# Attention copies ahead of the exponentials, and a filter's vector steps dealt more thinly over a projection

## The chip, the cores and the metric

One Trainium2 chip, one of its cores. The metric is the device time of one execution in microseconds (us). All data are float32. The engines are named as the profile names them: PE (TensorE), DVE (VectorE), ACT (ScalarE), POOL (GpSimd), SP (SyncE, here used to issue transfers).

## The reference

Two residual blocks run one after the other on x (1 x 2048 x 1024).

```
# first block
h = rmsnorm(x); q, k, v, g_a, u_p, g_p = split(h @ w_in)
a = banded_attention(q, k, v, rel_bias, sink) * silu(g_a)   # 8 heads, 2 kv heads, 128-token blocks, 3 blocks of keys
p = multiscale_pool(u_p) * silu(g_p)
x = x + rmsnorm(concat(a, p) @ w_out)
# second block
h = rms_norm(x); x0, x1, v (short conv of 3 taps), hy_gate, sg_u, sg_v, sg_gate = split(h @ w_in_2)
f = sin(fr1 * (z @ w1 + b1)); f = sin(fr2 * (f @ w2 + b2)); f = sin(fr3 * (f @ w3 + b3)); k = filter from f @ w_o
y_a = x0 * long_conv(v * x1, k) * silu(hy_gate)
y_b = sg_u * (per-head 128x128 mix of normalised sg_v) * silu(sg_gate)
x = x + rms_norm(concat(y_a, y_b) @ w_out_2)
```

The frequencies of the filter's sines are large, so its second layer (64 inputs, 64 outputs, 2048 positions) is computed in compensated float32 arithmetic on DVE, not on PE. The third layer is a matmul, behind the second layer's sine.

## The kernel before, in words

The stages follow one another: normalisation and projections of the first block; attention; output product of the first block; the values of the gating unit in the second block; the tiles of the second block's projection; the long convolution; the output product. Everything is one hand-written program for each engine, ordered by semaphores.

**Attention.** There are 32 steps `STEPS`, one for each block of 128 queries and each group of four heads. PE's program for step st, in order, is: two heads' probabilities turned (`turned(0)`, `turned(1)`, transposes at L859, behind `probs_done`), the products with the values of step st-1 (`products`, L880), two more heads turned, and the scores of step st+3 (`scores`, L783). DVE's is: `softmax_out(st)` (L682 to L685, it divides by the sums and ends with the long multiply of L685), `softmax_in(st+2)` (four reads of scores, L666, then the negated maxima, L670 and L671) and `gate(st-2)` (L693). ACT copies the turned probabilities out of PSUM, one copy for each of four heads (L535), and computes the exponentials of step st+2 (`exponentials`, four at L471 with their sums and a small one at L473). The turned heads share two PSUM banks, so a head is turned only when the copy of the head two before it is done.

**The projection's tiles.** A list `tiles` is walked by all engines. First, for h of 0 to 7: `gate` h, `mix` h, `u` h. Then, for e of 0 to 7: `x0` e, `hgate` e, `x1` e, `v` e; the tile `third` (the filter's third layer) stands in this list too. All but `mix` and `third` are projection tiles: 96 matmuls of 512 columns (L1836 to L1838) into four PSUM banks, two sets of banks taking turns. So tile j needs the banks of tile j-2 (`banks_free`) and its low weights WL. DVE makes the low weights of the tile two ahead (L1721) behind its own work on tile j: two products for `mix` (L1767, L1771), one for `u` (L1762) and `hgate` (L1778), two outer taps for `x0`, `x1` and `v` (L1731, L1734), a product more for `v` (L1775). Before that, ACT empties the tile (Silu, or the middle tap of L1706) and makes the high weights (L1663).

Behind its own work on a tile, DVE does some of the 631 steps of the filter's second layer, each on 128x1024 elements (L120 to L143): `SV_OPS` deals 60 of them to the stage before, and `OPS_BY` says how many go behind each kind of tile. At one tile DVE does all that are left and then `second_angle` (L1739 to L1741 and `reduce_angle`), for which ACT's sine (L1674) and then the tile `third` (L1820) wait. Behind `third` DVE does `third_angle` (L1745 to L1749), and ACT two sines (L1677, L1678) ahead of its work on `hgate` 7.

In the first 24 tiles there is a chain of transfers too: when DVE has done `u` h, SP stores it (L1631, 1 MB), and only then does POOL load the values of `mix` h+1 (L1657, 1 MB) into the same part of SBUF.

Of the kernel before, what the change touches and what calls it, by code (L numbers as in the profile page):

```python
# [13 lines left out]
P = 128  # L14
# [60 lines left out]
def OPS_OF(rows):  # L75

    return 10 * rows - 9
# [73 lines left out]
def first_block(nc, ctx, A, M, WOH, WOL, FH, FL, PS, kept, x1_d, h1_d, h2_d, wv_d):  # L151
# [60 lines left out]
    def turned_keys(slot, r, n):  # L212
        base, step = ((45056 + 2 * W_KEYS * (r % 2), W_KEYS), (47616 if r % 2 else 31744, 832 if r % 2 else W_KEYS))[slot]
        return M[:, base + step * (r // 2):base + step * (r // 2) + n]
# [98 lines left out]
    def keys_of(n):  # L313
        return [kb for kb in (n - 1, n, n + 1) if 0 <= kb < NT]

    def cols_of(n):
        ks = keys_of(n)
        return (ks[0] - n + 1) * P, (ks[-1] - n + 2) * P

    STEPS = [(n, g) for n in range(NT) for g in range(2)]  # L320
# [128 lines left out]
    def first_scalar(s, ahead_of_scale, ahead_of_square, behind_square):  # L449
# [15 lines left out]
        def exponentials(st):  # L465
            n, g = STEPS[st]
            c0, c1 = cols_of(n)
            st_sm = SM[:, st % 3]
            s.wait_ge(negmax_done, st + 1)
            for r in range(4):  # L470
                s.activation(SC[:, st % 3, r, c0:c1], SC[:, st % 3, r, c0:c1], ACT.Exp,  # L471
                             bias=st_sm[:, 1, r:r + 1], accum_out=st_sm[:, 2, r:r + 1]).then_inc(exp_done, 1)
            s.activation(st_sm[:, 3], st_sm[:, 3], ACT.Exp).then_inc(exp_done, 1)  # L473
# [42 lines left out]
        def weights_high(k):  # L516
            s.activation(WOH[:, k], WOL[:, k].bitcast(F32), ACT.Copy).then_inc(woh_done, 1)

        def features_high(i):
            s.wait_ge(attn_done, 2 * i + 2)  # L520
            s.wait_ge(pt_in[i % 2], 16 * (i // 2 + 1))
            if i >= 2:
                s.wait_ge(mix_done, i - 1)
            s.activation(FH[:, i % 2, 0:4], GA[:, :, P * i:P * i + P], ACT.Copy).then_inc(fh_done, 1)
            s.activation(FH[:, i % 2, 4:8], FL[:, i % 2, 4:8].bitcast(F32), ACT.Copy).then_inc(fh_done, 1)

        for st, (n, g) in enumerate(STEPS):
            for r in range(4):
                if r == 2 and st + 2 < len(STEPS):
                    exponentials(st + 2)  # L530
                s.wait_ge(pT_done, 4 * st + r + 1)
                if st >= 2:
                    s.wait_ge(pv_done, st - 1)
                nk = P * len(keys_of(n))
                s.activation(turned_keys(st % 2, r, nk), PS[:, 4 + r % 2, 0:nk], ACT.Copy).then_inc(pT_read, 1)  # L535
            if st == len(STEPS) - 2:
                s.wait_ge(wo_in, 16 * KD)
                s.wait_ge(scores_done, len(STEPS))
                features_high(0)
                weights_high(0)  # L540
# [623 lines left out]
def second_inputs(nc, A, PS, first, first_ctx, CC, HP, kept, h1_d, h2_d, vn_d, bi_d, u_d, gx_d, yb_d, wv_d):  # L1164

    with ExitStack() as outer:
# [75 lines left out]
        def rows_behind(sp, a, n):  # L1242

            for q in range(a, min(a + n, OPS_OF(HID))):
                r = row_used_by(q)
                if r is not None and r + 4 < ROWS_OF(HID):
                    row_load(sp, r + 4)
            return min(a + n, OPS_OF(HID))

        w_cols = []  # L1250
        tiles = []
        for h in range(8):
            tiles += [("gate", h, 6144 + P * h), ("mix", h, None), ("u", h, 4096 + P * h)]
        for e in range(8):
            if e == 7:
                tiles.append(("third", 0, None))
            tiles += [("x0", e, P * e), ("hgate", e, 3072 + P * e), ("x1", e, 1024 + P * e), ("v", e, 2048 + P * e)]
        weights = [j for j, t in enumerate(tiles) if t[2] is not None]
        slot_of = {j: w for w, j in enumerate(weights)}
        wv2 = A["w_in_2"].rearrange("(k p) e -> p k e", p=P)  # L1260
# [5 lines left out]
        with ExitStack() as ctx:  # L1266
# [18 lines left out]
            STEPS = 2 * NT  # L1285
# [284 lines left out]
        with ExitStack() as ctx:  # L1570
# [26 lines left out]
            third = tiles.index(("third", 0, None))  # L1597
            NV = 8

            def evacs_before(j):  # L1600

                return sum(t[0] not in ("u", "mix") for t in tiles[:j])
# [8 lines left out]
            def _(sp):  # L1611
                values_sync(sp)

                def raw_next(w):
                    if w + 2 < len(weights):
                        sp.wait_ge(wl_done, NV + w + 1)
                        weight_load(sp, w + 2)
# [10 lines left out]
                for j, (kind, n, _) in enumerate(tiles):  # L1628
# [9 lines left out]
                    if j in slot_of and slot_of[j] + 2 < len(weights):  # L1638
                        raw_next(slot_of[j] + 2)
                    a = rows_behind(sp, a, OPS_BY[kind])  # L1640

# [18 lines left out]
            def _(s):  # L1660
# [8 lines left out]

                values_scalar(s, first_high)  # L1670
                for j, (kind, n, _) in enumerate(tiles):
                    if j == third - 1:
                        s.wait_ge(arg2_done, 1)
# [39 lines left out]
            def _(v):  # L1713
# [10 lines left out]
                def outer_taps(which, n, j):  # L1724

                    conv = 3 * n + which
                    ps = PS[:, 4 * (j % 2):4 * (j % 2) + 4, :].rearrange("p a b -> p (a b)")
                    dst = AB[CONV_AT[CONV[which]]]
                    w = CW[:, 8 * which + n]
                    v.wait_ge(evac_done, evacs_before(j) + 1)  # L1730
                    v.scalar_tensor_tensor(out=dst[:, 1:S], in0=ps[:, 0:S - 1], scalar=w[:, 0:1], in1=dst[:, 1:S],  # L1731
                                           op0=ALU.mult, op1=ALU.add).then_inc(tap_step, 1)
                    v.wait_ge(tap_step, conv + 1)
                    v.scalar_tensor_tensor(out=dst[:, 0:S - 1], in0=ps[:, 1:S], scalar=w[:, 2:3], in1=dst[:, 0:S - 1],  # L1734
                                           op0=ALU.mult, op1=ALU.add).then_inc(taps_done, 1)
                    v.wait_ge(taps_done, conv + 1)
# [6 lines left out]
                def third_angle(j):  # L1743
                    v.wait_ge(evac_done, evacs_before(j) + 1)
                    link(v.tensor_scalar(L3[0], L3[0], VEC3[:, 0:1], VEC3[:, 1:2], ALU.add, ALU.mult))  # L1745
                    v.wait_ge(tile_done, j + 1)
                    reduce_angle(link, v, L3[0], L3[1], L3[2])
                    v.tensor_scalar(L3[1], L3[1], -3.1415925, 3.1415925, ALU.max, ALU.min).then_inc(arg3_done, 1)
                    v.memset(L3[2][HID:P, 0:1], 0.0).then_inc(arg3_done, 1)  # L1749
# [7 lines left out]
                for j, (kind, n, _) in enumerate(tiles):  # L1757
                    ps = PS[:, 4 * (j % 2):4 * (j % 2) + 4, :].rearrange("p a b -> p (a b)")
                    if kind == "u":
                        v.wait_ge(tile_done, j + 1)  # L1760
                        v.wait_ge(mix_gated, n + 1)
                        v.tensor_tensor(AB[n % 2], ps, AB[n % 2], ALU.mult).then_inc(sgu_done, 1)  # L1762
                    elif kind == "mix":
                        v.wait_ge(tile_done, j + 1)
                        v.wait_ge(sgt_in[n % 2], 32 * (n // 2 + 1))
                        psb = PS[:, 4 * (j % 2):4 * (j % 2) + 4, :].rearrange("p a (b c) -> p (a b) c", c=P)
                        v.scalar_tensor_tensor(out=psb, in0=psb, scalar=NW[:, n:n + 1], in1=BI[:, n % 2].unsqueeze(1).to_broadcast([P, NT, P]),  # L1767
                                               op0=ALU.mult, op1=ALU.add).then_inc(mix_biased, 1)
                        v.wait_ge(mix_biased, n + 1)
                        v.wait_ge(evac_done, evacs_before(j))  # L1770
                        v.tensor_tensor(AB[n % 2], ps, AB[n % 2], ALU.mult).then_inc(mix_gated, 1)  # L1771
                    elif kind in CONV:
                        outer_taps(CONV.index(kind), n, j)
                        if kind == "v":
                            v.tensor_tensor(AB[1], AB[0], AB[1], ALU.mult).then_inc(u_done, 1)  # L1775
                    elif kind == "hgate":
                        v.wait_ge(evac_done, evacs_before(j) + 1)
                        v.tensor_tensor(AB[0], AB[0], AB[1], ALU.mult).then_inc(gx_done, 1)  # L1778
                    elif kind == "third":
                        third_angle(j)  # L1780
                    if j in slot_of and slot_of[j] + 2 < len(weights):
                        weights_low(slot_of[j] + 2)
                    if (kind, n) == ("x0", 6):
                        filter_work(v, OPS_OF(HID))
                        second_angle()
                    else:
                        filter_work(v, OPS_BY[kind])
                v.wait_ge(sin3_done, 2)
# [53 lines left out]


SV_OPS = [0] * 8 + [3] * 20 + [0] * 4
OPS_BY = {"gate": 12, "u": 13, "mix": 6, "x0": 13, "hgate": 13, "x1": 13, "v": 13, "third": 0}


def reduce_angle(link, v, x, out, tmp):
# [1006 lines left out]
```

## Time and profile before

| | before |
|---|---|
| median of 3 runs | 3157.5 us (3156.0 to 3157.89) |
| the profiled execution: its time | 3156.89 us |
| the profiled execution: its span | 3154.8 us |
| PE, DVE, ACT busy in the span | 2986.2, 2543.4, 814.3 us |
| attention, start of the first L685 to start of the last | 578.9 to 736.2 us |
| the projection's tiles, first matmul to last | 1144.9 to 2259.6 us |

Busy time is the time in which an engine has an instruction in flight; PE's matmuls overlap, so a busy PE is not a PE at its fastest. The distance from one matmul's start to the next tells more. A row's idle time stands in brackets, with what ended it.

### The profile page before, as it was taken

The page shows a single profiled execution, that of the slowest core. Times are in us where ns is not written, and L with a number is a line of the kernel's source. Part 1 is how long each engine was busy: PE and PEld are TensorE (multiplying, and loading weights), DVE is VectorE, ACT ScalarE, POOL GpSimd, SP SyncE. Part 2 cuts the span into 40 slices and gives each one's busy share as a digit, 9 for nine tenths or more (in the row PEclk, how much of TensorE's full clock was granted, in tenths as well). Part 3 has the DMA queues.
Part 4 walks back from the last instruction along what each step waited for, and adds up shares of the span by engine and source line. Part 5 has one row for each costly group of instructions (what it writes and reads, how often), then busy time and mean ns, then how long its engine had stood idle before and what let it go on. Part 6 is the DMA issues. An engine that isn't in the chain of part 4 may idle for free. (4 is left out here: it accounts for less than half of the span.)

```text
span 3154.8 us, 32979 instructions
## 1 busy us (share of the span) xinstructions
PE 2986.2 (95%) x12866; PEld 2164.8 (69%) x12866; DVE 2543.4 (81%) x2789; ACT 814.3 (26%) x1370; POOL 336.1 (11%) x458
## 2 busy tenths in 40 slices
PE   8999999889998999999999999998889989889999
PEld 4444444656777888888888887776656656678887
DVE  7979999898996869999999999996368879762121
ACT  3000000585334220000011111111344626631111
POOL 2212121001343430000000000000000000000000
PEclk9999999999999999999999999999999999999999
DMA  7675552201457546565555445431222331453331
GB/s 213 182 179 149 172 151 73 114 1 57 143 186 237 146 135 167 157 184 153 155 140 140 127 140 147 134 100 47 97 91 66 123 112 56 147 167 115 99 107 41
DMA packets 212116, 406.39 MB, mean 129 GB/s; under 512 B 21009, under 2 KB 134329, under 8 KB 204089
## 3 DMA queue, kind: packets, MB, share of 16 engines
q1 hardware_dynamic: 189256, 324.58, 34.0%
q0 software_dynamic: 21552, 71.32, 8.3%
q10 hardware_dynamic: 1152, 8.39, 0.7%
q8 instruction: 102, 1.67, 0.2%
q14 instruction: 54, 0.43, 0.0%
HBM read 324.53 MB, written 85.98 MB: 130 GB/s over the span
## 5 line engine op out<-in xcount | busy, mean ns | idle before, releaser
L1836 PE MATMUL PS<-HX,WH 128*128 128x512 f32 x1536 | 602.4, 392 | 23.1 <-DVE WL L1721 15.1
L1838 PE MATMUL PS<-HX,WL 128*128 128x512 f32 x1536 | 600.0, 391 | 0.0
L1837 PE MATMUL PS<-HX,WH 128*128 128x512 f32 x1536 | 599.9, 391 | 0.0
L843 PE MATMUL PS<-M 128*128 128x512 f32 x1088 | 472.0, 596 | 7.6 <-DVE M L644 6.4
L843 PEld LDWEIGHTS PS<-M 128*128 128x128 f32 x1088 | 207.4, 191 | 272.0 <-issue 263.7
L1836 PEld LDWEIGHTS PS<-HX,WH 128*128 128x128 f32 x1536 | 290.0, 189 | 88.3 <-issue 15.8
L1838 PEld LDWEIGHTS PS<-HX,WL 128*128 128x128 f32 x1536 | 289.8, 189 | 60.7
L1837 PEld LDWEIGHTS PS<-HX,WH 128*128 128x128 f32 x1536 | 290.0, 189 | 59.7
L120 DVE SCALAR_TENSOR_TENSOR HP<-MF,HP 128x1024 f32<-128x1024 f32 x252 | 323.4, 1283 | 8.0
L120 DVE SCALAR_TENSOR_TENSOR M<-M 128x1024 f32<-128x1024 f32 x160 | 205.5, 1285 | 26.6 <-DMA M<-c_feat 21.1
L2523 PE MATMUL PS<-WH,YH 128*128 128x512 f32 x512 | 201.9, 394 | 9.3 <-DVE HP L2662 5.2
L2524 PE MATMUL PS<-WH,YL 128*128 128x512 f32 x512 | 200.9, 392 | 0.0
L2525 PE MATMUL PS<-WL,YH 128*128 128x512 f32 x512 | 200.9, 392 | 0.0
L2646 DVE TENSOR_TENSOR YL<-KX,YH 128x2048 fp32r<-128x2048 f32 x14 | 32.1, 2291 | 206.7 <-ACT YH L2625 206.7
L1706 ACT ACTIVATE MB<-PS,MF 128x2048 f32<-128x2048 f32 x24 | 49.6, 2065 | 475.2 <-PE PS L1838 392.2
L2053 POOL DMA_DIRECT2D M<-c_decay x48 | 25.8, 538 | 1112.5 <-DVE KX L2167 909.0
L72 POOL DMA_DIRECT2D M<-c_feat x186 | 94.9, 515 | 382.6 <-DVE M L120 361.9
L2523 PEld LDWEIGHTS PS<-WH,YH 128*128 128x128 f32 x512 | 97.3, 190 | 31.7 <-issue 7.1
L1521 PE MATMUL PS<-WVH,HX 128*128 128x512 f32 x256 | 102.5, 400 | 13.9 <-DVE HX L1445 6.0
L1020 DVE TENSOR_TENSOR M<-M 128x1024 f32<-128x1024 f32 x90 | 110.1, 1223 | 2.4
L2525 PEld LDWEIGHTS PS<-WL,YH 128*128 128x128 f32 x512 | 97.1, 190 | 20.6
L2524 PEld LDWEIGHTS PS<-WH,YL 128*128 128x128 f32 x512 | 97.4, 190 | 20.0
(223 smaller groups left out, 5048.9 us busy)
## 6 DMA issues: line engine op xcount, KB each, us to landing
MF<-h_scratch SPq DMA_DIRECT2D x380, 256.0 KB, 4.3
M<-c_feat POOLq DMA_DIRECT2D x186, 256.0 KB, 4.4
MF<-w_in SPq DMA_DIRECT2D x52, 512.0 KB, 4.8
M<-u_scratch SPq DMA_DIRECT2D x16, 1024.0 KB, 4.8
M<-c_decay POOLq DMA_DIRECT2D x48, 256.0 KB, 2.9
M<-x SPq DMA_DIRECT2D x18, 512.0 KB, 4.2
M<-w_in SPq DMA_DIRECT2D x18, 512.0 KB, 5.5
x_scratch<-M SPq DMA_DIRECT2D x16, 512.0 KB, 5.1
```

The costliest lines, as they stand in the source:

```text
L72: eng.dma_start(dst[HID * half:HID * half + HID], row).then_inc(loaded, 16)
L120: return v.scalar_tensor_tensor(out=out, in0=a, scalar=s_, in1=b, op0=op0, op1=op1)
L843: ins = t.matmul(ps[:, c, :], wt[:, k], HT[:, k, TC * c:TC * c + TC], start=(k == 0), stop=(k == KD - 1))
L1020: link(v.tensor_tensor(out, a, b, op))
L1521: t.matmul(dst, hh, wh, start=(k == 0), stop=False)
L1706: s.activation(AB[CONV_AT[kind]], ps, ACT.Identity, bias=w[:, 3:4], scale=w[:, 1:2]).then_inc(evac_done, 1)
L1836: t.matmul(dst, wh, hh, start=(k == 0), stop=False)
L1837: t.matmul(dst, wh, hl, start=False, stop=False)
L1838: ins = t.matmul(dst, wl, hh, start=False, stop=(k == KD - 1))
L2523: t.matmul(dst, yh, wh, start=(n == 0), stop=False)
L2524: t.matmul(dst, yl, wh, start=False, stop=False)
L2525: return t.matmul(dst, yh, wl, start=False, stop=(n == KY - 1))
```

## The change

Two things are changed. In attention, ACT makes all four copies of a step and then the exponentials of step st+2; before, the exponentials stood between the second copy and the third. In the projection, `u`, `x0` and `x1` take 12 filter steps instead of 13, `v` takes 11 and `hgate` 14. The tile at which DVE does what is left, and then the second angle, is `x1` 6 instead of `x0` 6. The tile `third` stands behind `x0` 7 instead of ahead of it.

```diff
@@ first_scalar
             for r in range(4):
-                if r == 2 and st + 2 < len(STEPS):
-                    exponentials(st + 2)
                 s.wait_ge(pT_done, 4 * st + r + 1)
                 if st >= 2:
                     s.wait_ge(pv_done, st - 1)
                 nk = P * len(keys_of(n))
                 s.activation(turned_keys(st % 2, r, nk), PS[:, 4 + r % 2, 0:nk], ACT.Copy).then_inc(pT_read, 1)
+            if st + 2 < len(STEPS):
+                exponentials(st + 2)
@@ second_inputs
         for e in range(8):
+            tiles.append(("x0", e, P * e))
             if e == 7:
                 tiles.append(("third", 0, None))
-            tiles += [("x0", e, P * e), ("hgate", e, 3072 + P * e), ("x1", e, 1024 + P * e), ("v", e, 2048 + P * e)]
+            tiles += [("hgate", e, 3072 + P * e), ("x1", e, 1024 + P * e), ("v", e, 2048 + P * e)]
@@
-                    if (kind, n) == ("x0", 6):
+                    if (kind, n) == ("x1", 6):
                         filter_work(v, OPS_OF(HID))
                         second_angle()
@@
-OPS_BY = {"gate": 12, "u": 13, "mix": 6, "x0": 13, "hgate": 13, "x1": 13, "v": 13, "third": 0}
+OPS_BY = {"gate": 12, "u": 12, "mix": 6, "x0": 12, "hgate": 14, "x1": 12, "v": 11, "third": 0}
```

## Rows read from the trace of the kernel before

**Rows 1.** Waits, 578 to 731 us: us in total, times, longest.
```profile
PE PS L859 <- ACT M L535: 19.6, 29, 1.7
DVE M L666 <- PE PS L783: 6.1, 14, 1.6
```
**Rows 2.** Timeline of ACT in one step: start, us, instruction, idle before.
```profile
703.25 0.62 ACT L471 ACTIVATE M<-M 128x384 f32<-128x384 f32 x1 [0.51 <-DVE M L671]
...
705.76 0.84 ACT L535 ACTIVATE M<-PS 128x384 f32<-128x384 f32 x2
```
**Rows 3.** Timeline of PE in the same stretch.
```profile
701.32 0.85 PE L859 MATMUL PS<-M 128*128 128x128 f32 x6 [0.79 <-ACT M L535]
...
703.54 0.87 PE L859 MATMUL PS<-M 128*128 128x128 f32 x6
704.34 1.56 PE L783 MATMUL PS<-M 64*128 64x384 f32 x8
```
**Rows 4.** Timeline of DVE in the same stretch.
```profile
698.81 1.76 DVE L685 TENSOR_TENSOR M<-M 128x1536 f32<-128x1536 f32 x1
...
703.87 1.76 DVE L685 TENSOR_TENSOR M<-M 128x1536 f32<-128x1536 f32 x1
705.95 0.62 DVE L666 CUSTOM_DVE_ANT_0 M<-PS,M 128x384 f32<-128x384 f32 x1 [0.33 <-PE PS L783]
```
**Rows 5.** Waits, 731 to 746 us.
```profile
DVE M L666 <- PE PS L783: 0.5, 1, 0.5
PE PS L859 <- ACT M L535: 2.4, 2, 1.8
```
**Rows 6.** Source view of L1767 (`mix`): first and last start.
```profile
L1767 DVE SCALAR_TENSOR_TENSOR PS<-PS,MF,MB x8: 2357/2359/2359, 1186.5 to 1529.9; 128x2048 f32<-128x2048 f32 x8
```
**Rows 7.** Timeline of DVE: twelve filter steps behind `gate` 0.
```profile
1171.05 1.22 DVE L143 TENSOR_TENSOR MF<-HP,MF 128x1024 f32<-128x1024 f32 x1
...
1186.53 2.36 DVE L1767 SCALAR_TENSOR_TENSOR PS<-PS,MF,MB 128x2048 f32<-128x2048 f32 x1
```
**Rows 8.** Source view of L1706 (ACT, middle tap), 1550 to 1820 us.
```profile
L1706 ACT ACTIVATE MB<-PS,MF x10: 2065/2067/2069, 1556.8 to 1817.9; 128x2048 f32<-128x2048 f32 x10
```
**Rows 9.** Source view of L1731 (DVE, first tap), 1740 to 2110 us.
```profile
L1731 DVE SCALAR_TENSOR_TENSOR MB<-PS,MF,MB x13: 2349/2349/2351, 1743.0 to 2104.4; 128x2047 f32<-128x2047 f32 x13
```
**Rows 10.** Timeline of PE: `mix` 1, `mix` 7 with the next tile, `x0` 0.
```profile
1216.31 0.91 PE L1813 MATMUL PS<-MB 128*128 128x128 f32 x6 [2.18 <-DMA MB<-vn_scratch]
...
1507.93 3.81 PE L1813 MATMUL PS<-MB 128*128 128x128 f32 x32 [0.28 <-DMA MB<-vn_scratch]
1511.50 0.47 PE L1836 MATMUL PS<-HX,WH 128*128 128x512 f32 x1
...
1534.68 0.50 PE L1836 MATMUL PS<-HX,WH 128*128 128x512 f32 x1 [1.15 <-DVE MB L1771]
```
**Rows 11.** Timeline of SP: the stores of `u` 0 and `u` 6.
```profile
1201.18 0.33 SPq L1631 DMA_DIRECT2D yb_scratch<-MB  x1
...
1495.45 0.34 SPq L1631 DMA_DIRECT2D yb_scratch<-MB  x1
```
**Rows 12.** Waits of PE, 1534.6 to 2163 us.
```profile
PE PS L1836 <- DVE WL L1721: 13.2, 6, 6.1
```
**Rows 13.** Timeline of PE: `third` and the tile behind it.
```profile
2163.14 1.97 PE L1820 MATMUL PS<-MF 64*64 64x512 f32 x16
2170.12 0.80 PE L1836 MATMUL PS<-HX,WH 128*128 128x512 f32 x1 [5.02 <-DVE MB L1734]
```
**Rows 14.** Timeline of DVE: second angle, third angle, what follows each.
```profile
2124.46 0.81 DVE L1739 TENSOR_SCALAR MF<-MF 128x1024 f32<-128x1024 f32 x1
...
2135.13 2.28 DVE L1778 TENSOR_TENSOR MB<-MB 128x2048 f32<-128x2048 f32 x1
...
2173.45 1.34 DVE L1745 TENSOR_SCALAR MF<-MF 128x2048 f32<-128x2048 f32 x1
...
2192.79 0.06 DVE L1749 MEMSET HP<- 64x1 f32 x1
```

## The prediction, as it was put on record

> **What bounds the kernel now.** The change touches two stretches, attention (578.9 to about 738 us) and the projection's tiles (1144.9 to 2259.6), so I read each by itself: first the waits of the stretch, then a timeline of each engine over one period, then the view of one instruction, whose first and last start give the length of a period.
>
> In attention the three engines are all nearly full. Two waits matter [rows 1]: PE waits for ACT's copies 29 times, 19.6 us in all, and DVE waits for PE's scores 14 times, 6.1 us in all. One period shows how they hang together. ACT computes exponentials from 703.25 to 705.76 and only then makes the copies of the third and fourth head [rows 2]. PE turns the next head only when such a copy is done: at 701.32 it had sat 0.79 us. From there to the end of its scores it takes 704.34 + 1.56 - 701.32 = 4.58 us, so to 705.90 [rows 3]. DVE ends its long multiply at 703.87 + 1.76 = 705.63 and starts on the scores at 705.95, after 0.33 idle [rows 4]. Without that idle time its period is 703.87 - 698.81 = 5.06 us. So DVE sets the pace, and every second step PE is a third of a microsecond late, because of ACT's order.
>
> In the projection the period of DVE and that of PE have to be compared. PE: ACT's first tap follows the end of a tile at once where PE is not held up, and x0 0 to x0 3 is 12 tiles in 1817.9 - 1556.8 = 261.1, so 21.76 a tile and 87.0 for the four tiles of an e [rows 8]. DVE: between the taps of x0 2 and of x0 6 lie four periods, (2104.4 - 1743.0) / 4 = 90.35 [rows 9]. DVE is the slower by 3.3 us an e; PE first eats its lead and then waits for low weights, 13.2 us in 6 waits [rows 12]. For the 24 tiles in front: DVE's period over an h is (1529.9 - 1186.5) / 7 = 49.06 [rows 6]; PE's is two tiles and a mix, 2 x 21.76 + (1511.50 - 1507.93) = 47.09 [rows 10]. Here too DVE is the slower, and x0 0 starts at 1534.68 behind the second product of mix 7, whose banks it needs [rows 10]. So through the projection the bound is DVE, until its filter steps run out; from there PE.
>
> **The change, part by part.**
>
> A filter step costs DVE (1186.53 - 1171.05) / 12 = 1.29 us [rows 7].
>
> First, u takes 12 instead of 13. DVE's period over an h falls to 47.77, still above PE's 47.09. Seven deals of u stand in front of mix 7's products, so they end 7 x 1.29 = 9.0 earlier, at 1525.7 by DVE alone. By PE alone it would be 1144.9 + 16 x 21.76 + 8 x 3.57 = 1521.6. A third limit is the chain u, store, load, mix. From the store's issue to the mix it took 1216.31 - 1201.18 = 15.1 at mix 1 and 1507.93 - 1495.45 = 12.5 at mix 7 [rows 10, 11]. Say PE ends gate h at 0. High and low weights are ready some 3.3 + 1.1 later (evacuation 2.1, high 1.1, low 1.1, the durations of like operations), twelve steps take 15.5, the two products 4.6, six steps 7.7, u's product 2.2: 34.5. With the chain behind it, mix h+1 may start at 47.0 to 49.6, where PE comes at 47.1. A mix that is late holds PE, but not DVE's steps, so the next chain starts no later and only every second wait is a new one. At a chain of 13.8 (the mean) this costs 1.5 us over the stretch beyond DVE's limit. I take x0 0 at 1527.2, 7.5 earlier. With all chains at 12.5 it is 9; with all at 15.1 PE's period is (47.1 + 49.6) / 2 = 48.4 and the gain is about 2.5.
>
> Second, the tiles of an e take 12 + 14 + 12 + 11 = 49 steps instead of 52. DVE's period becomes 90.35 - 3 x 1.29 = 86.5, below PE's 87.0: PE is the bound, and does not wait for weights any more. What it lost is the distance between two of its own rows less the tiles in it: from 1534.68 to third at 2163.14 [rows 10, 13] stand 28 tiles, 28 x 21.76 = 609.3 of 628.5. The loss was 19.2 us (15 of idle time, 4 of matmuls at twice their distance behind it, TensorE's lower clock). I count all of it as gained. If DVE kept some lag, it would be less; the margin is 0.5 us an e, so I put the lower bound at 12.
>
> Third, the steps left over. Before: 8 x 31 + 6 x 52 = 560 of the 571 that the tiles have to do, so 11 at x0 6. After: 8 x 30 + 6 x 49 + 12 + 14 = 560, so 11 at x1 6. PE ends x1 6 at 1527.2 + 27 x 21.76 = 2114.7. DVE: first tap at 2116.9, both taps to 2121.7, low weights of x0 7 at 2122.8, eleven steps to 2137.0, second angle (2135.13 - 2124.46 = 10.7 [rows 14]) to 2147.7. Before, it was the next tile but one that wanted weights queued behind the angle, 6.1 us of wait [rows 12]; now DVE has little lag, and the weights of x0 7 stand ahead of the eleven steps. Queued behind the angle are v 6's taps (to 2152.4) and the sine of ACT; third comes at 2114.7 + 2 x 21.76 = 2158.2. So 5.8 us of cover, and it costs nothing.
>
> Fourth, third behind x0 7. Before, the tile behind third waited for the taps of v 6, which PE had just finished: 2170.12 - 2163.14 = 7.0 from third's start [rows 13]. Now hgate 7 waits for the taps of x0 7 in the same way: the same 7.0, and the slow matmuls behind it too. Nothing gained, nothing lost. Third angle (2192.79 - 2173.45 = 19.3 [rows 14]) now ends at 2158.2 + 7.0 + 1.1 + 19.3 = 2185.6, ACT's two sines at about 2189.7, as PE ends hgate 7 at 2189.0. Its emptying is late by a microsecond; who waits for it is the last v, by its banks and low weights, from 2211 on. Cover: 15 us. SP's row loads move with the steps; each is issued a dozen steps ahead as before.
>
> Fifth, attention. With the copies first, PE can begin a pass at the end of the probabilities, 700.57 instead of 701.32, and its scores end at 705.2, 0.4 before DVE wants them. I count DVE's waits for scores, less the 1.6 us one in front, which is behind another tile: 4.5, and 0.5 at the end [rows 1, 5]. At the end PE loses another 1.8 us to ACT [rows 5]; there the last exponentials come 1.3 later but PE starts earlier: I take 1.0 of 0 to 2. What waits now is the exponentials. From the start T of a pass, heads three and four are turned from T + 2.2 to 3.1 (703.54 [rows 3]), copied to T + 3.9, exponentials to T + 6.4. DVE asks for them at T + 7.8: cover 1.4. Behind them stand the first two copies of the next step, ready at T + 6.9 and 7.3; PE wants them for its third and fourth head at T + 5.1 + 2.2 = 7.3 and 7.7. Cover 0.4, the tightest place. Sum 6.0 us, bounds 0 and 7.5.
>
> **Sum.** 7.5 + 19.2 + 6.0 = 32.7. The profiled execution took 3156.9 (2.1 around its span of 3154.8), so 3124.2; the median of the runs is 0.6 above it. Prediction 3125. Between the stretches and behind them nothing hangs on a fixed time, so what is gained stays.
>
> **Rivals.**
>
> The chain of transfers decides in the first 24 tiles. For it: it varies by 2.6 us, and row loads run beside it. Against: at mix 7 it took 12.5 and the wait was 0.28 [rows 10]. It gives 15.1 throughout, a gain of 2.5 for 7.5, so 3130. The Trainium skill ("DMA: Bandwidth & Descriptors", Issuing engines are not separate DMA queues) says that transfers of SP and POOL end on the same 16 DMA engines and interleave. By that rule the row loads, hardly fewer than before, keep slowing POOL's load, and this rival is the outcome.
>
> Attention gains nothing: the cover of 0.4 is not there and the step stays at 5.2 on average. 3131.
>
> DVE stays the bound in the e tiles: 12 instead of 19.2 is gained there. 3132; together with one of the others some 3137.
>
> Slower: ACT's exponentials behind the copies become attention's bound. Each microsecond that the first copies come later than PE wants them is one in each of 30 steps. To undo 26.7 it takes 0.9 a step, so copies 1.3 later than reckoned; at 1.2 a step it is 3157.5 - 26.7 + 36 = 3167. Against: ACT's own loop is 2.5 of exponentials and 1.7 of copies, with some 0.4 between, 4.6 of the 5.06.
>
> **How the numbers follow.** Forecast 0.70 (3125; its own range 3120 to 3130), chain 0.11 (3130), attention without gain 0.08 (3131), DVE still the bound 0.07 (3132 to 3137), slower 0.03 (3167), and 0.01 for no change. The range is 3119 to 3134. A measurement of this kernel tells some 0.2% (6 us) from no change. Faster by more 0.95, within 0.02, slower 0.03.
>
> **What would show it.** DVE's idle time before L666 gone and L685 every 5.06 us; PE's waits for low weights gone between x0 0 and third; ACT's first taps every 87.0 for an e up to x1 6; x0 0 near 1521 (attention's 6 less); third some 33 us earlier and a wait of 5 behind it. Wrong would be a PE that waits for copies in attention, or for L1721 again, or longer for vn_scratch.

## The result, and the profile after

The changed kernel takes 3132.3 us (median of 4 runs, 3128.7 to 3135.0), against 3156.75 us before in the same comparison (4 runs, 3155.8 to 3157.9). The ratio is 0.9922, with a 95% interval of 0.9905 to 0.9939: 24 us, or 0.8%, faster. Forecast were 3125 and a range of 3119 to 3134.

The profiled execution took 3128.7 us, with a span of 3126.9. Line numbers of the projection and behind it are one higher than before, and the copies of turned probabilities are L533 instead of L535. Attention's waits, in the stretch that answers to [rows 1]:

```profile
ACT M L533 <- PE PS L859: 26.4, 32, 1.4
PE PS L859 <- DVE M L685: 12.8, 30, 1.6
...
DVE M L666 <- PE PS L783: 1.6, 1, 1.6
```

But for 0.3 us once, TensorE no longer waits for ACT's copies in this stretch. ACT waits for TensorE, TensorE for the probabilities of VectorE, and VectorE for scores only once, at the start. The pace is in the view of the probabilities' multiply L685: 25 of them, first and last start.

```profile
L685 DVE TENSOR_TENSOR M<-M x25: 1757/1757/1759, 604.3 to 722.8; 128x1536 f32<-128x1536 f32 x25
```

That is (722.8 - 604.3) / 24 = 4.94 us a step (4.96 each, the last one 4.43). The same 25 of the kernel before:

```profile
L685 DVE TENSOR_TENSOR M<-M x25: 1757/1757/1759, 604.9 to 729.2; 128x1536 f32<-128x1536 f32 x25
```

5.18 a step. The first 24 tiles of the projection: TensorE's waits in the kernel before, then in the changed one, and the view that answers to [rows 6]:

```profile
PE PS L1813 <- DMA MB<-vn_scratch: 7.1, 6, 2.5
PE PS L1836 <- DVE MB L1771: 2.9, 4, 1.2
```

```profile
PE PS L1814 <- DMA MB<-vn_scratch: 6.8, 7, 1.8
PE PS L1837 <- DVE WL L1722: 1.9, 1, 1.9
```

```profile
L1768 DVE SCALAR_TENSOR_TENSOR PS<-PS,MF,MB x8: 2359/2359/2359, 1176.3 to 1514.1; 128x2048 f32<-128x2048 f32 x8
```

The waits for VectorE's mix product are gone, but all seven mixes with a predecessor waited for the stored values, and the period is (1514.1 - 1176.3) / 7 = 48.26, not VectorE's 47.77 of the prediction. In the e tiles (ACT's and VectorE's first taps, as [rows 8] and [rows 9]):

```profile
L1707 ACT ACTIVATE MB<-PS,MF x10: 2065/2067/2069, 1542.2 to 1803.4; 128x2048 f32<-128x2048 f32 x10
```

```profile
L1732 DVE SCALAR_TENSOR_TENSOR MB<-PS,MF,MB x13: 2349/2350/2351, 1719.1 to 2067.2; 128x2047 f32<-128x2047 f32 x13
```

TensorE's 12 tiles take 261.2, and VectorE's period is (2067.2 - 1719.1) / 4 = 87.03: both are at TensorE's pace now. From 1541 to 2152 us TensorE has no wait at all. The only one behind it in the projection is that of the tile after `third`, as [rows 13]:

```profile
PE PS L1837 <- DVE MB L1735: 5.0, 1, 5.0
```

By first instructions the profiled execution gained 10.2 us up to the projection (its first matmul 1144.94, now 1134.72) and 22.8 in the projection, so the convolution starts 33.0 earlier (2269.64, now 2236.61). Then 5.2 are given back: from there to the output's first matmul it takes 504.0 instead of 498.8. Behind that the kernels take the same 386.

### The profile page after: what moved, and what is told of

The parts are those of the page before. It is cut to its first block and busy times, and to the rows that moved or that the text cites. A ratio compares the mean times of both kernels' runs of the same rounds, so it can differ in the third digit from the quotient of the medians.

```text
span 3126.9 us, 32982 instructions
## 1 busy us (share of the span) xinstructions
PE 2980.9 (95%) x12866; PEld 2162.9 (69%) x12866; DVE 2541.6 (81%) x2789; ACT 811.2 (26%) x1370; POOL 335.9 (11%) x458
## 3 DMA queue, kind: packets, MB, share of 16 engines
q8 instruction: 102, 1.67, 0.2%
## 5 line engine op out<-in xcount | busy, mean ns | idle before, releaser
L72 POOL DMA_DIRECT2D M<-c_feat x186 | 94.9, 515 | 382.6 <-DVE M L120 361.9
```

The costliest lines, as they stand in the source:

```text
L72: eng.dma_start(dst[HID * half:HID * half + HID], row).then_inc(loaded, 16)
```

## The experiments

Each comparison below is with the kernel before in runs on the same chip. To keep the parts apart I name for most runs the time from the projection's first matmul to ACT's first tap of x0 0, called the **first part** (411.8 before, 407.5 in the changed kernel's first profile), and the length of the convolution.

**Attention alone.** Before, with this:

```
             for r in range(4):
-                if r == 2 and st + 2 < len(STEPS):
-                    exponentials(st + 2)
...
+            if st + 2 < len(STEPS):
+                exponentials(st + 2)
```

> Only the attention's part of the change. My theory: the gain is DVE's, whose period falls from 5.21 on average to 4.96 us, so the projection's first matmul comes 10.2 us earlier than before (8.6 of it by the end of attention), and the kernel takes 3146 to 3148 us. Rival (the 10.2 are shared with the projection's stage, which starts from another point): 6 us, 3151. If the long convolution loses TensorE clock by where it happens to start, as it did in the changed kernel (5.1 us), the time can be up to 5 us above the theory's with the projection still 10.2 us earlier.

3149.97 us (10 runs; before 3157.45), ratio 0.9978 (0.9969 to 0.9987). The step is 4.94 us as in the changed kernel. Counted from the first scores, the first matmul of attention's output projection comes 8.4 us earlier than before (8.3 in the changed kernel's profile). Counted from the first probabilities, the projection's first matmul comes 9.7 earlier, between the 10.2 of the theory and the 6 of the rival. The projection was as before (first part 412.1). The median is 2 us above the theory's range. In this profile the convolution took 501.6 us, 2.8 more than before, which the expectation had allowed for.

**Projection alone.** The tile order, the place of the second angle and the deals, with attention as before:

```
         for e in range(8):
+            tiles.append(("x0", e, P * e))
             if e == 7:
                 tiles.append(("third", 0, None))
...
-                    if (kind, n) == ("x0", 6):
+                    if (kind, n) == ("x1", 6):
...
-OPS_BY = {"gate": 12, "u": 13, "mix": 6, "x0": 13, "hgate": 13, "x1": 13, "v": 13, "third": 0}
+OPS_BY = {"gate": 12, "u": 12, "mix": 6, "x0": 12, "hgate": 14, "x1": 12, "v": 11, "third": 0}
```

> Only the projection's part. Theory: the stage from its first matmul to its last becomes 22.8 us shorter, 4 of it ahead of x0 0 and 19.2 behind it, and DVE never makes PE wait for low weights; the convolution starts 22.8 us earlier, the kernel takes 3134 us. Rival: with a late convolution clock, 3134 to 3139. If the parts helped each other, their gains alone would add up to less than 33.0 at the start of the convolution.

3137.73 us (4 runs; before 3157.45), ratio 0.9939 (0.9924 to 0.9954). The first part took 410.0 and the whole projection 1103.2 instead of 1124.7. TensorE waited 9.3 us for the stored values. Expected were 22.8 us in the projection, 4 of it in the first part; it was 21.5, with 1.8 in the first part. The two parts' ratios add to 0.83%, about the 0.78 of the whole.

**The thinner deals without the moved angle and layer.** Attention as changed, new deals, `third` ahead of x0 7 and the second angle at x0 6, where all leftover steps now fall. The deals are those of the edit above, and SP's row loads follow the leftover:

```
-                    a = rows_behind(sp, a, OPS_BY[kind])
+                    a = rows_behind(sp, a, OPS_OF(HID) if (kind, n) == ("x0", 6) else OPS_BY[kind])
```

> Attention's part and the thinner deals, but DVE does what is left (37 steps instead of 11) and the second angle at x0 6 still, and third stays ahead of x0 7; SP issues the rows of all those steps there. Theory: what was spread is paid back in one wait. 26 steps more than before, 33.5 us, stand ahead of the low weights of v 6, with only the lag gained as cover: a wait of some 27 us at v 6 instead of 6, the projection's stage 3 us longer to 1 us shorter than before, the kernel 3145 to 3150 us. Rival (thinner deals alone bring the gain, and the place of the angle is of no matter): 3128 to 3133.

3160.1 us (10 runs; before 3157.45), ratio 1.0012 (1.0002 to 1.0021), with attention's gain in it. Its waits of TensorE from 1134 to 2275 us:

```profile
PE PS L1836 <- DVE WL L1721: 29.0, 2, 27.1
PE PS L1813 <- DMA MB<-vn_scratch: 10.3, 6, 2.5
```

The steps that were taken off the tiles pile up at one tile, with the angle behind them, and the weights of the next tile but one come 27.1 us late in one wait, as expected. But the kernel is 10 us above the expected 3145 to 3150. Its projection, from its first matmul to the convolution's, is 10.3 us longer than before (1135.0 for 1124.7) instead of 3 at most: the first part took 412.5 and gained nothing, and the matmuls behind the long wait ran at twice their distance. The deals save time only if the leftover has a tile with room for it.

**Third layer ahead of x0 7 again,** all the rest as changed:

```
         for e in range(8):
-            tiles.append(("x0", e, P * e))
             if e == 7:
                 tiles.append(("third", 0, None))
+            tiles.append(("x0", e, P * e))
```

> The changed kernel with the third layer ahead of x0 7 again, all the rest as changed: second angle at x1 6, new deals. If the later angle needs the third layer one tile later, TensorE waits at the third layer for the sine: the angle is ready about a tile and a half before, so 10 to 18 us are lost there, the half clock behind the wait costs 2 to 3 more, and the kernel takes 3142 to 3155. Rival, the order of these two tiles is worth nothing (the sine is ready in time either way): 3130 to 3135, and no wait of TensorE on the sine over 1 us.

3147.74 us (4 runs; before 3158.26), ratio 0.9957 (0.994 to 0.9973). Its waits of TensorE from 1138 to 2262 us:

```profile
PE PS L1821 <- ACT MF L1675: 12.5, 1, 12.5
PE PS L1814 <- DMA MB<-vn_scratch: 11.6, 4, 3.4
```

The sine is waited for 12.5 us, and the sixteen short matmuls behind that wait take 3.29 us where they took 1.97 [rows 13]. So moving the third layer by a tile is needed as soon as the angle is later. The rest of this run's time is the other wait, and the profile shows its rhythm in mixes 1 and 3:

```profile
1209.78 5.24 PE L1814 MATMUL PS<-MB 128*128 128x128 f32 x32 [2.44 <-DMA MB<-vn_scratch]
...
1308.95 3.25 PE L1814 MATMUL PS<-MB 128*128 128x128 f32 x15 [3.27 <-DMA MB<-vn_scratch]
```

Mix 2 between them had no wait: only every second late chain is a new one. And the 32 matmuls behind the first wait take 5.24 us, where they take 3.81 at the full clock [rows 10]. So it is with all four mixes that waited (5.15 to 5.44 us), 5.8 us in all. This run's first part took 417.4 us, ten more than the changed kernel's, by the same code up to there.

**The chain of transfers taken off the path.** The changed kernel with other deals:

```
-OPS_BY = {"gate": 12, "u": 12, "mix": 6, ...
+OPS_BY = {"gate": 12, "u": 18, "mix": 0, ...
```

The six steps between the mix's products and u's product go behind u's product, so u is stored up to six steps (7.7 us) earlier, with the same work ahead of the next mix's products.

> The changed kernel with mix 0 and u 18 instead of mix 6 and u 12: the six steps stand behind u's product, so its store and the load of the next mix's values start some 7 us earlier, and DVE has as much to do as before. Theory (in the changed kernel the chain of transfers, not DVE, sets the pace of the first 24 tiles): PE's seven waits for vn_scratch go, x0 0 starts 3 to 5 us earlier, the kernel 3 to 5 us shorter. Rival (DVE sets it): the waits for vn_scratch turn into waits for DVE and nothing is gained.

3124.91 us (4 runs; before 3157.45), ratio 0.99 (0.9883 to 0.9916). The first part took 405.2, 2.3 us less than in the changed kernel's first profile (expected were 3 to 5). The waits for stored values are gone, and a small one on VectorE's mix product is there instead. Run again:

> The version with no filter steps at a mix tile and 18 at a u tile once more, beside the next two: 3122 to 3128, and a projection of 1099 us from its first matmul to the convolution's first. If only the convolution's share moves between executions, the projection stays within 0.7 us of 1099.2 and the convolution lies anywhere from 498 to 505.

3122.76 us (4 runs; before 3157.94), ratio 0.9888 (0.9872 to 0.9905), first part 405.2 and the projection 1099.2 both times, and the convolution 499.1 and 499.3. So the expectation held. TensorE's wait in the second one:

```profile
PE PS L1837 <- DVE MB L1772: 4.2, 7, 0.8
```

**One step fewer at u, and its step dealt to hgate.**

```
-OPS_BY = {"gate": 12, "u": 12, "mix": 6, "x0": 12, "hgate": 14, ...
+OPS_BY = {"gate": 12, "u": 17, "mix": 0, "x0": 12, "hgate": 15, ...
```

> The changed kernel with deals of 0 at mix, 17 at u (12 at gate as before), 15 at hgate. In the version with 18 at u TensorE waited 4.1 us in 7 waits for VectorE's mix product, and for no transfer. If VectorE's work is what bounds the first 24 tiles there (29 steps of 1.29 us a group in place of 30), these waits go, 3.5 to 4.1 us less up to x0 0, and no wait on the stored values appears as there is still about 18 us of cover for 15: 3118 to 3124. Rival, the transfers are next: VectorE comes to the mix product 1.3 us earlier, the row is waited for instead, and 0 to 1 us is gained: 3122 to 3128.

3121.13 us (4 runs; before 3157.94), ratio 0.9882 (0.9867 to 0.9897), the fastest kernel here (the next one, with 3121.47, is as fast within the noise). Its first part took 399.0 us, 12.9 less than before. The products of the mix stand 47.19 us apart, TensorE's own period (47.09) but for 0.1:

```profile
L1768 DVE SCALAR_TENSOR_TENSOR PS<-PS,MF,MB x8: 2359/2359/2360, 1180.1 to 1510.4; 128x2048 f32<-128x2048 f32 x8
```

and in the whole first part TensorE has one wait left, for the first low weights (1.9 us). SP stores u 0 at 1188.26 and the mix begins at 1207.50, with no wait before it:

```profile
1188.26 0.33 SPq L1632 DMA_DIRECT2D yb_scratch<-MB  x1
```

```profile
1207.50 3.73 PE L1814 MATMUL PS<-MB 128*128 128x128 f32 x32
```

So 19.2 us from the store's issue to the mix, where the changed kernel had 14.2 and a wait of 1.25:

```profile
1190.95 0.33 SPq L1632 DMA_DIRECT2D yb_scratch<-MB  x1
```

```profile
1205.14 3.81 PE L1814 MATMUL PS<-MB 128*128 128x128 f32 x32 [1.25 <-DMA MB<-vn_scratch]
```

Against the version with 18 at u the first part is 6.2 us shorter (expected were 3.5 to 4.1), but only 2.6 of it are left at the convolution: x0 0 to `third` takes 1.9 longer, by a wait of 1.8 for v 6's taps, and the tile behind `third` waits 7.3 instead of 5.0. Those taps stand behind the second angle in VectorE's queue, and VectorE gets no sooner through its steps because TensorE is ahead (this is read from the order of the queue; no run moved the angle here).

**The same with 13 steps at x0,** which leaves 5 for the angle's tile instead of 12.

> The same with 13 steps at x0 instead of 12, which leaves 5 for the tile of the second angle instead of 12. If the wait of 5.0 us of TensorE behind VectorE's taps late in the projection comes from the leftover steps and the angle, it shrinks to 0 to 2 us and the kernel gains 3 to 5 us on the one before it; if VectorE has no room for a 51st step in a group of four tiles, TensorE waits 1.3 us in each and the gain is gone again: 3118 to 3128.

3121.47 us (4 runs; before 3157.94), ratio 0.9882 (0.9868 to 0.9897): no change. The wait behind `third` is 7.0 instead of 7.3, so a smaller leftover does not shorten it. VectorE has the same number of steps up to the angle however they are dealt.

**Exponentials behind three copies.**

```
             for r in range(4):
+                if r == 3 and st + 2 < len(STEPS):
+                    exponentials(st + 2)
                 s.wait_ge(pT_done, 4 * st + r + 1)
...
-            if st + 2 < len(STEPS):
-                exponentials(st + 2)
```

> The changed kernel with the exponentials of a step behind three copies of the step before instead of behind all four. Theory of the prediction, what counts is that the copies of turned probabilities don't queue behind the exponentials: TensorE waits for the fourth copy at the end of the exponentials once a step, so the gain is a part only, a step of 5.0 to 5.3 us, the last probabilities 0 to 4 us later than in the changed kernel (152.0 us from first to last there, 157.3 before), and the end of attention up to 3 us later still by the fourth copy of the last step but one. Whole 3127 to 3135. Rival, any place behind the second copy will do: 152.0 us and 8.6 us gained by the output of attention, as in the changed kernel, whole as there.

3157.54 us (10 runs; before 3157.94), ratio 0.9997 (0.9988 to 1.0006). Both expectations missed, by over 20 us. The step is neither 4.94 nor 5.2:

```profile
L685 DVE TENSOR_TENSOR M<-M x26: 1224/1757/1759, 606.7 to 753.5; 128x1536 f32<-128x1536 f32 x25, 128x1024 f32<-128x1024 f32 x1
```

(753.5 - 606.7) / 25 = 5.87, and the long steps take 5.92. ACT, one step of it:

```profile
696.11 0.49 ACT L535 ACTIVATE M<-PS 128x384 f32<-128x384 f32 x1 [1.44 <-PE PS L859]
696.49 0.61 ACT L471 ACTIVATE M<-M 128x384 f32<-128x384 f32 x1
...
698.98 0.84 ACT L535 ACTIVATE M<-PS 128x384 f32<-128x384 f32 x2
700.09 0.49 ACT L535 ACTIVATE M<-PS 128x384 f32<-128x384 f32 x1 [0.26 <-PE PS L859]
```

TensorE and VectorE in the same stretch (the three waits return in every step):

```profile
697.82 0.55 PE L859 MATMUL PS<-M 128*128 128x128 f32 x3
699.50 0.55 PE L859 MATMUL PS<-M 128*128 128x128 f32 x3 [1.14 <-ACT M L535]
```

```profile
697.93 0.62 DVE L666 CUSTOM_DVE_ANT_0 M<-PS,M 128x384 f32<-128x384 f32 x1 [0.87 <-PE PS L783]
```

ACT waits 1.44 for the third head to be turned, starts 2.5 us of exponentials in front of the fourth copy, and TensorE can't turn the next step's second head until that copy has emptied the bank that the two share. So TensorE's next scores are late by 1.14, VectorE waits 0.87 for them, and its maxima and the exponentials behind them are late in turn: a closed ring of three engines. In the kernel before, ACT began its exponentials as soon as VectorE's maxima let it, at 703.25 [rows 2], and had both late copies behind them; here it waits for the third head first, and everything behind is later by that. From the first probabilities to the projection's first matmul it takes 566.0 us with exponentials behind two copies, 583.1 behind three, and 556.0 to 557.1 behind four (the changed kernel's two profiles; 564.1 to 566.0 and 556.0 to 558.9 over all profiles with two and with four).

**The changed kernel once more.**

> The changed kernel as it is, once more, for the convolution. In its profile 17 to 18 of the 128 first-stage matmuls of the filter columns ran at 0.85 us instead of 0.43, against 7 in the kernel before, and the convolution took 504.0 us against 498.8. Theory A, the granted clock falls by where the kernel happens to stand in time, and differs from execution to execution: another count of slow matmuls in this profile, and a convolution of 499 to 507 us. Theory B, the loss belongs to the new kernel: the same counts by chunk, 4, 4, 5, 4, and 503.7 to 504.3 us.

3128.02 us (2 runs; before 3158.26), ratio 0.99 (0.988 to 0.992). The convolution took 499.2, not 504.0, with 0, 5, 5, 5 slow matmuls in its four chunks. (Counted are distances over 0.7 us between the 32 matmuls of a chunk; in the second to fourth chunk a wait of 2.3 us counts as one of them, so a 1 means that none was slow.) The same code took 4.8 us less in another execution, so the loss is not the code's own. Windows of TensorE over the convolution: stretch, its length, busy time and instructions, granted clock, DMA share, GB/s. First profile of the changed kernel:

```profile
2236.00:2284.00 48.00, 41.18 (x190) 0.90 0.46 176
...
2364.00:2390.00 26.00, 21.06 (x64) 0.93 0.06 21
2390.00:2492.00 102.00, 95.20 (x488) 0.98 0.34 120
...
2646.00:2741.00 95.00, 82.72 (x371) 0.94 0.37 133
```

The same kernel in this run:

```profile
2240.00:2288.00 48.00, 40.71 (x193) 0.93 0.50 187
...
2368.00:2394.00 26.00, 21.57 (x71) 0.93 0.07 21
2394.00:2496.00 102.00, 94.62 (x494) 1.00 0.34 120
...
2650.00:2741.00 91.00, 79.15 (x347) 0.96 0.37 134
```

Three of the four stretches shown got more clock. In the second one, the first stage of the second chunk, both lost it, and the kernel before, which stood elsewhere in time, did not:

```profile
2397.00:2423.00 26.00, 21.39 (x80) 1.00 0.07 21
```

**The convolution shifted in time,** by VectorE operations at the projection's end that write a tile nobody reads any more, four of them in the changed kernel, then two in the kernel before:

```
                 v.wait_ge(sin3_done, 2)
+                for _ in range(4):
+                    link(v.tensor_tensor(MISS, ACC, ACC, ALU.add))
```

> The changed kernel with four VectorE operations of 1.26 to 1.32 us more at the end of the projection, behind the wait for the third sine, where the convolution waits for them: they write a tile that nobody reads any more. Both theories: the convolution's first matmul 5.0 to 5.3 us later than in the changed kernel. Theory A, the loss hangs on where in time the convolution stands: the counts of slow matmuls by chunk change, and the convolution takes 497 to 503 us or over 505. Theory B, the loss belongs to the kernel's new code: 4, 4, 5, 4 stay, the convolution takes 503.7 to 504.3 us and the whole 3133 to 3140.

3140.79 us (2 runs; before 3158.26), ratio 0.9941 (0.9921 to 0.996). The shift itself was 4.7 us, a little under the expected 5.0 to 5.3. The slow matmuls are 4, 1, 4, 1 and the convolution took 501.5, which theory A allows and B does not. The rest of the loss is in the first part, 413.0 us in this run.

> The kernel before with two VectorE operations more at the same place, 2.5 to 2.6 us in all. Both theories: first matmul of the convolution 2.5 to 2.6 us later. Theory A: counts of slow matmuls other than 4, 1, 1, 1, and a convolution that is up to 5 us longer than 498.8, the whole up to 3165. Theory B: 4, 1, 1, 1 stay, 498.5 to 499.1 us, and the whole 3160.

3160.56 us (8 runs; before 3158.26), ratio 1.0008 (0.9998 to 1.0019). Shifted by 2.1 us (expected 2.5) the kernel before has the counts 0, 5, 5, 4, as the changed one had in other runs, yet a convolution of 499.2: what the first stage lost, other stretches won. Over the 14 profiles of this study the convolution took 498.7 to 504.0 us, and 504.0 came once, in the first profile of the changed kernel.

## Why the prediction came out as it did

Faster was right, and both medians of the changed kernel, 3132.3 and 3128.0, lie in the range of 3119 to 3134, 7 and 3 us above the forecast. The mechanism was right for attention and for the e tiles. In the first 24 tiles it was not: there the rival held.

**Attention, forecast 6.0 (0 to 7.5): 8.5 in the first two profiles, some 7.2 against the others.** That DVE sets the pace and loses its waits was right. The step was taken as 5.06 and is 4.96: in the kernel before DVE began to read the scores 1.77 us after the start of its multiply even where no wait is listed (698.81 to 700.58), and in the changed kernel after 1.67. The last probabilities are 5.4 us earlier (730.82, before 736.20), 5.2 counted from the first ones, against a forecast of 4.5 and 0.5 at the end. For the end itself, "I take 1.0 of 0 to 2", 3.1 us came (first matmul of the output product 736.73, before 745.24). In the kernel before the last exponentials stood in front of the third and fourth copy of the last step but one. TensorE of the kernel before, then of the changed one:

```profile
736.27 0.72 PE L859 MATMUL PS<-M 128*128 128x128 f32 x4 [1.82 <-ACT M L535]
736.92 2.15 PE L880 MATMUL PS<-M 128*64 128x256 f32 x12
739.00 2.27 PE L859 MATMUL PS<-M 128*128 128x128 f32 x8
```

```profile
732.10 0.66 PE L859 MATMUL PS<-M 128*128 128x128 f32 x4 [0.69 <-DVE M L685]
732.69 1.08 PE L880 MATMUL PS<-M 128*64 128x256 f32 x8
734.14 0.71 PE L859 MATMUL PS<-M 128*128 128x128 f32 x4 [0.37 <-ACT M L533]
```

I had counted the 1.8 of idle time, but not that the products of that step came behind it, nor the slow matmuls that followed it: 12 take 2.15 us, where in the middle of attention they take 1.52, and 8 take 2.27 where four take 0.71 in the changed kernel. These slow matmuls belong to that execution and not to the order of the copies. In the run of the kernel before with a shifted convolution the wait is the same 1.82 and the 12 stand at full clock:

```profile
736.87 0.72 PE L859 MATMUL PS<-M 128*128 128x128 f32 x4 [1.82 <-ACT M L535]
737.52 1.52 PE L880 MATMUL PS<-M 128*64 128x256 f32 x12
```

From the last probabilities to the first matmul of the output product it takes 9.0 us in the profile of before, but 7.8 in the two other profiles with the old order, and 5.9 with the new one. So the end is worth 1.9, inside the bounds of 0 to 2, and 1.2 of the 3.1 was the clock's. Of the 10.2 us at the projection's first matmul the other 1.7 are not attention's: nearly all of them came between 930 and 1010 us. There the matmuls of the profile of before stood 0.43 us apart up to 962.8, and their counterparts in that of after 0.23 (granted clock 0.93 from 960 to 980 us, and 1.00 from 951 to 971). From the first probabilities to the projection's first matmul the lead is 10.0 in this profile, 9.7 with attention alone changed, and 8.9 in the repeated run.

The rival that exponentials behind the copies become the bound did not come about: over all of attention TensorE waited for a copy in front of a head twice, 0.3 and 0.4 us. But the run with three copies shows how near such a loss lies: exponentials and one copy in the other order, 1.0 us a step, 26 us from the first to the last probabilities.

**First 24 tiles, forecast 7.5: 4.3 in the first profile, and 0.5 on average.** This is the step that failed. The deals of 12, 12 and 6 ran in seven profiles, with the first part at 407.5, 408.4, 410.0, 412.1, 412.5, 413.0 and 417.4, a mean of 411.6. The kernel before and the two runs with its deals had 411.8, 412.1 and 412.2. "At a chain of 13.8 (the mean) this costs 1.5": 13.8 was right for the kernel before, where the seven chains from the store's issue to the mix have a mean of 13.6. But with the new deals the mean is 14.9 in the best profile and 16.1 in the worst, so the deals' gain was eaten by the transfer. The rival "the chain of transfers decides" (chance 0.11, a gain of 2.5) was what happened, and on average it cost still more than the rival said. One detail of the reckoning was right, "only every second wait is a new one", and it is the rhythm of the run at 417.4. What had no term at all are slow matmuls behind these waits: 5.8 of the 10 us between the best and the worst profile. VectorE's own term was too high as well. With 18 at u and 0 at mix, as many steps in all, TensorE waits for VectorE and no longer for the transfers, and the gain is 6.6 of the 9.0 reckoned for it. With one step fewer and the chain covered 12.9 were to be had.

Of the DMA view, the loads of the stored values into MB (1 MB each by POOL's queue; last figure the median from issue to landing), changed kernel:

```profile
MB<-vn_scratch POOLq DMA_DIRECT2D x7, 1024.0 KB, 9.1
```

Before it was 7.6, and 9.1 to 10.3 in all seven profiles with the new deals: the chain did not stay in its old range. The rule of the Trainium skill that the prediction named ("DMA: Bandwidth & Descriptors", Issuing engines are not separate DMA queues) has it that transfers of SP and POOL interleave on the same 16 engines, from which the prediction took that the row loads slow POOL's load. The traces agree, and show which rows. The load for mix 1 and SP's row loads (L72, 256 KB each) in the changed kernel, where the load took 9.3 us:

```profile
1193.28 13.99 SPq L72 DMA_DIRECT2D MF<-h_scratch  x8
1195.73 1.17 POOL L1658 DMA_DIRECT2D MB<-vn_scratch  x1 [46.04 <-DMA yb_scratch<-MB]
```

The same with 17 at u, where it took 7.3 and the first row load follows it by 4.1 us:

```profile
1192.91 1.17 POOL L1658 DMA_DIRECT2D MB<-vn_scratch  x1 [39.49 <-DMA yb_scratch<-MB]
1197.00 15.30 SPq L72 DMA_DIRECT2D MF<-h_scratch  x10
```

In the first case 2.4 MB moved while the load was under way, in the second 1.8, at 263 and 248 GB/s. Over all 98 such loads of the 14 profiles, the 19 with no row load issued from 3.9 us before to 2.1 after them took 6.8 to 7.8 us, and the 44 with four took 8.1 to 11.5 (these bounds were chosen with the traces at hand). So the thinner deals changed when SP's row loads are issued, and the load met more of them. That is read from traces; no run moved the row loads alone. With 18 at u and 0 at mix the load took 7.2 to 7.3; with 17, 9.0 again in the median, but there 19.2 us from store to mix hid it.

**The e tiles, forecast 19.2: 19.0.** No wait of TensorE from x0 0 to `third`, and 28 tiles from the start of x0 0 have lost 0.2 us where they had lost 19.2. The bound from both engines' periods, 86.5 against 87.0, held. **The leftover steps and the second angle, forecast nothing: nothing**, and the two runs without one or the other place show 27.1 and 12.5 us where the cover is gone. **Third layer behind x0 7, forecast 7.0 for 7.0: 7.0** (2151.41 to 2158.40), and two slow matmuls more behind it, 0.5 us.

**"Between the stretches and behind them nothing hangs on a fixed time, so what is gained stays."** The convolution's length moves by up to 5 us with TensorE's clock, and the range said nothing of it. The first profile of the changed kernel has the longest one of all 14. The matmuls of the second chunk that answer to each other, kernel before and after, both behind an equal wait:

```profile
2415.05 3.74 PE L2335 MATMUL PS<-M 128*128 128x512 f32 x8 [2.33 <-DVE M L2184]
```

```profile
2382.52 5.30 PE L2336 MATMUL PS<-M 128*128 128x512 f32 x8 [2.33 <-DVE M L2185]
```

The same eight matmuls, 1.6 us apart. On average this costs the change little: the seven profiles with its deals have a convolution of 500.7 us, the three with the old deals 499.9. With the first part's 10 us of scatter it can account for one profile that shows the forecast 33 us at the convolution, and medians that show 24 and 30; runs without a profile can't be taken apart, so this is not shown. In the first profile attention's 8.5 for 6.0, 1.7 of luck behind it, 4.3 for 7.5, 19.0 for 19.2 and the 0.5 behind `third` met at 33.0 for 32.7. So the agreement of the sum there is luck, and proves nothing for its parts.

## What to carry to other kernels

A deal of one engine's steps decides when its other results leave, so read how long the store and the load behind them take at their slowest, and put the steps behind the result that has the longest way. Of an operation that moves along a queue, price each place by itself: behind two, three and four copies were 566, 583 and 556 us, and no line through two of them gives the third. And judge a forecast of a few microseconds term by term over several profiles, because a right sum can be made of wrong terms. A load's time read from a trace holds only as long as what runs beside it stays where it was.

## What the runs showed of the hardware

- TensorE's granted clock in a stretch of 26 us of the convolution was 1.00 in one kernel and 0.93 in the other, with the same work and the same gaps of 1.4 to 2.3 us around it. At the lower of its two levels (1.2 instead of 2.4 GHz) the 128x512 matmuls stood 0.85 us apart instead of 0.43, in steps of some 1.6 us of loss. The repeat of one and the same kernel gained such a step in three places. What decides it in an execution stays open; the repeat only shows that the code alone doesn't.
- A load of 1 MB took 7.2 to 7.7 us from issue to landing in some deals and 9.0 to 10.3 in others, with 156 to 164 GB/s moved over the stretch in all of them. (These are medians of a profile's seven; single loads took 6.3 to 11.8 us.) It is long where another queue's loads of 256 KB are issued around it: with four of them 8.1 to 11.5 us, with none 6.8 to 7.8.
- Behind a wait for a transfer, the 32 matmuls of a mix (128x128) took 5.2 to 5.4 us in nine mixes of these profiles, with waits of 2.0 to 3.4 us, and 3.8 in others with waits of up to 2.7. Such a wait can cost 1.4 us more than its own length.
